# Attention heads one by one, or in pairs with wider operations

## The reference, cut to what matters

```
s = jnp.einsum('bqkgd,bskd->bkgqs', qi, ki).astype(F32) * scale
s = jnp.where(mi[None, None, None], s, -jnp.inf)
sink_col = jnp.broadcast_to(sink[None, :, :, None, None], s.shape[:-1] + (1,))
p = jax.nn.softmax(jnp.concatenate([s, sink_col], axis=-1), axis=-1)[..., :-1]
return jnp.einsum('bkgqs,bskd->bqkgd', p.astype(vi.dtype), vi)
```

## Time and profile before

| | |
|---|---|
| median of 3 runs | 1547.64 us |
| profiled execution, time | 1549.7 us |
| its span, first to last instruction | 1547.9 us |
| mean granted clock of TensorE | 0.962 |
| busy share of the span | PE 96%, PEld 81%, DVE 83%, ACT 64%, POOL 4% |
| attention, first score matmul to first matmul of the output projection | 458.81 to 510.34 us |

### The profile page before, as it was taken

How to read it: one execution, slowest core, us unless ns; L and a number is a source line. 1 busy time by engine, 2 the same in 40 slices (tenths; PEclk the granted TensorE clock), 3 DMA queues, 4 the chain that set the end, 5 groups by cost and what they waited for, 6 DMA issues and landing times.

```text
span 1547.9 us, 19150 instructions
## 1 busy us (share of the span) xinstructions
PE 1489.5 (96%) x7536; PEld 1247.8 (81%) x7537; DVE 1290.3 (83%) x1542; ACT 991.1 (64%) x1191; POOL 62.8 (4%) x57
## 2 busy tenths in 40 slices
PE   7998899999889979999999999999999999999996
PEld 5887799999545868888888888888888888888885
DVE  5488798988558448799999999999999999999995
ACT  2152344344327248788888888888888888888884
POOL 0000000000000030001001001001001000000001
PEclk7799999999988969999999999999999999999998
DMA  9875969989640529999999999999999999999980
GB/s 341 300 253 198 327 228 313 326 312 329 217 179 1 181 78 350 373 330 361 393 383 364 395 384 354 397 386 369 391 386 366 385 392 361 384 395 375 375 300 16
DMA packets 222159, 485.46 MB, mean 314 GB/s; under 512 B 6160, under 2 KB 33008, under 8 KB 222064
## 3 DMA queue, kind: packets, MB, share of 16 engines
q1 hardware_dynamic: 217296, 474.04, 83.5%
q0 software_dynamic: 2160, 7.87, 2.0%
q10 hardware_dynamic: 2608, 2.27, 0.4%
HBM read 477.86 MB, written 6.29 MB: 313 GB/s over the span
## 4 chain that ended last, share of the span: by engine, by line
issue 51%; PE 38%; DVE 6%; POOL 3%; ACT 1%; DMA 0%; ACTq 0%; DVEq 0%; POOLq 0%
PE bank L1534 5%; PE bank L1535 4%; PE bank L1536 4%; PE bank L1728 3%; PE bank L1729 3%; PE bank L1730 3%; PE bank L1459 2%; PE bank L1442 2%; PE bank L1594 2%; PE bank L1426 1%; POOL y L598 1%; PE bank L1411 1%; PE bank L1357 1%; PE bank L1401 1%; POOL out L602 1%
## 5 line engine op out<-in xcount | busy, mean ns | idle before, releaser
L1298 DVE TENSOR_TENSOR wlo<-ring,whi 128x1024 fp32r<-128x1024 f32 x672 | 815.1, 1236 | 77.8 <-ACT whi L858 55.9
L858 ACT ACTIVATE whi<-ring 128x1024 fp32r<-128x1024 f32 x672 | 711.7, 1062 | 178.5 <-PE bank L1730 178.3
L1728 PE MATMUL bank<-whi,xh 128*128 128x512 f32 x904 | 360.3, 399 | 4.2 <-DVE wlo L1298 3.9
L1730 PE MATMUL bank<-wlo,xh 128*128 128x512 f32 x904 | 354.3, 392 | 0.0
L1729 PE MATMUL bank<-whi,xl 128*128 128x512 f32 x904 | 353.8, 391 | 0.0
L1728 PEld LDWEIGHTS bank<-whi,xh 128*128 128x128 f32 x904 | 170.7, 189 | 41.3 <-issue 7.8
L1730 PEld LDWEIGHTS bank<-wlo,xh 128*128 128x128 f32 x904 | 170.7, 189 | 36.7
L1729 PEld LDWEIGHTS bank<-whi,xl 128*128 128x128 f32 x904 | 171.1, 189 | 33.9
L1728 PE MATMUL bank<-whi,hh 128*128 128x512 f32 x440 | 172.0, 391 | 0.0
L1730 PE MATMUL bank<-wlo,hh 128*128 128x512 f32 x440 | 171.3, 389 | 0.0
L1729 PE MATMUL bank<-whi,hl 128*128 128x512 f32 x440 | 171.2, 389 | 0.0
(11 more groups left out here) (254 smaller groups left out, 1671.1 us busy)
## 6 DMA issues: line engine op xcount, KB each, us to landing
ring<-in_m_w_gu SPq DMA_DIRECT2D x112, 2048.0 KB, 10.9
ring<-in_m_w_down SPq DMA_DIRECT2D x56, 2048.0 KB, 10.5
ring<-in_ada_w SPq DMA_DIRECT2D x24, 2048.0 KB, 12.8
ring<-in_f_w_gu SPq DMA_DIRECT2D x24, 1024.0 KB, 14.1
ring<-in_f_w_down SPq DMA_DIRECT2D x6, 2048.0 KB, 14.4
ring<-in_a_w_in SPq DMA_DIRECT2D x4, 2048.0 KB, 17.2
ring<-in_kv_ada_w SPq DMA_DIRECT2D x4, 2048.0 KB, 13.1
ring<-in_a_w_out SPq DMA_DIRECT2D x2, 2048.0 KB, 10.3
```

The source lines that it names most:

```text
L858: nc.scalar.activation(whi[:, n % WB, :], moe_raw(n), ACT.Copy).then_inc(hi_ready, 1)
L1298: v_.tensor_tensor(wlo[:, n % WB, :], moe_raw(n), whi[:, n % WB, :].bitcast(F32), ALU.subtract).then_inc(lo_ready, 1)
L1728: mm(o, hi, whi[:, b, c0:c0 + 512], start=start, stop=False)
L1730: return mm(o, hi, wlo[:, b, c0:c0 + 512], start=False, stop=stop)
```

## The change

Heads are handled in pairs, p = 0 to 7. Each DVE `scores` of a pair is four `tensor_tensor_reduce` (scale, mask and running maximum with the sink as the start value, straight from PSUM), one negation and one addition of the sinks for both heads; `probs` is four instructions for both heads, the multiplications as `tensor_tensor` with the reciprocal broadcast. DVE's order is `probs(p)`, `scores(p+2)`, then the copy of `values(p-1)`, which moves from ACT to DVE. ACT does the four exponentials of a pair without waits between them, one sink exponential and one copy of 768 columns from two banks. PE issues four `keep_clock` ahead of the scores of each pair, also ahead of the first, then the four score matmuls with the two heads (two halves of the partitions, two banks) taking turns; the `keep_clock` between scores and transposes are gone. `Pb` becomes three buffers of a pair, `PT` moves into `G`, and the transposes have one pair of banks (4, 5), so `probs_T(p)` waits for `copy_p(p-1)`. Scores use banks 0 to 3, values banks 6 and 7.

The diff, with its added lines; what they replace are the functions printed above:

```diff
@@ -128,7 +128,8 @@
...
+        psum = ctx.enter_context(nc.psum_tensor("psum", [P, 8, 512], F32))
+        bank = [psum[:, i, :] for i in range(8)]
...
@@ -168,7 +169,10 @@
...
+        flat = lambda t: t[:, :, :].rearrange("p k n -> p (k n)")
+        Pb = [part.rearrange("p (b n) -> p b n", b=2) for part in (
+            flat(Dd)[:, 0:6 * P], flat(Dd)[:, 6 * P:12 * P], flat(C)[:, 0:6 * P])]
+        PT = flat(G)[:, 0:12 * P].rearrange("p (b n) -> p b n", b=4)
...
@@ -500,6 +505,8 @@
...
+        score_bank = lambda p, j: bank[2 * (p % 2) + j]
...
@@ -761,35 +768,30 @@
...
+            ex, pt = Signal(exp_done), Signal(pT_evac)
+            def exps(p):
+                act.wait_ge(nm_done, p + 1)
+                for j in range(2):
+                    h = 2 * p + j
+                    nc.scalar.activation(Pb[p % 3][:, j, 0:P], Pb[p % 3][:, j, 0:P], ACT.Exp, bias=nm[:, h, 0:1],
+                                         accum_out=sm[:, h, 0:1])
+                    nc.scalar.activation(Pb[p % 3][:, j, P:3 * P], Pb[p % 3][:, j, P:3 * P], ACT.Exp,
+                                         bias=nm[:, h, 1:2], accum_out=sm[:, h, 1:2])
+                act.wait_ge(es_set, p + 1)
+                then(nc.scalar.activation(es[:, 2 * p:2 * p + 2, :], es[:, 2 * p:2 * p + 2, :], ACT.Exp), ex)
+            def copy_p(p):
+                act.wait_ge(pT_mm, p + 1)
+                if p >= 2:
+                    act.wait_ge(pv_mm, p - 1)
+                then(nc.scalar.activation(PT[:, 2 * (p % 2):2 * (p % 2) + 2, :], psum[:, 4:6, 0:3 * P], ACT.Copy), pt)
...
+            for p in range(NH // 2):
+                if p + 1 < NH // 2:
+                    exps(p + 1)
+                copy_p(p)
...
@@ -1179,32 +1181,48 @@
...
+            sce, nms, ess, pns, oe = (Signal(sc_evac), Signal(nm_done), Signal(es_set), Signal(pn_done),
+                                      Signal(o_evac))
+            def scores(p):
+                dve.wait_ge(sc_mm, p + 1)
+                if p >= 3:
+                    dve.wait_ge(pT_mm, p - 2)
+                pair = slice(2 * p, 2 * p + 2)
+                for j in range(2):
+                    h = 2 * p + j
+                    for c0, c1, i in ((0, P, 0), (P, 3 * P, 1)):
+                        ins = v_.tensor_tensor_reduce(out=Pb[p % 3][:, j, c0:c1], in0=score_bank(p, j)[:, c0:c1],
+                                                      in1=mask[:, c0:c1], scale=HD ** -0.5, scalar=sinks[:, h:h + 1],
+                                                      op0=ALU.add, op1=ALU.max, accum_out=mx[:, h, i:i + 1])
+                then(ins, sce)
+                then(v_.tensor_scalar(nm[:, pair, :], mx[:, pair, :], -1.0, None, ALU.mult), nms)
+                then(v_.tensor_tensor(es[:, pair, :], nm[:, pair, :], sinks[:, pair][:, :, None].to_broadcast([P, 2, 2]),
+                                      ALU.add), ess)
+            def probs(p):
+                pair = slice(2 * p, 2 * p + 2)
+                dve.wait_ge(exp_done, p + 1)
+                then(v_.tensor_tensor(sm[:, pair, :], sm[:, pair, :], es[:, pair, :], ALU.add))
+                then(v_.reciprocal(sm[:, pair, :], sm[:, pair, :]))
+                for c0, c1, i in ((0, P, 0), (P, 3 * P, 1)):
+                    ins = v_.tensor_tensor(Pb[p % 3][:, :, c0:c1], Pb[p % 3][:, :, c0:c1],
+                                           sm[:, pair, i:i + 1].to_broadcast([P, 2, c1 - c0]), ALU.mult)
+                then(ins, pns)
+            def copy_o(p):
+                dve.wait_ge(pv_mm, p + 1)
+                then(v_.tensor_copy(A[:, p, :], bank[6 + p % 2][:, 0:SEQ]), oe)
+            for p in range(2):
+                scores(p)
+            for p in range(NH // 2):
+                probs(p)
+                if p + 2 < NH // 2:
+                    scores(p + 2)
+                if p:
+                    copy_o(p - 1)
+            copy_o(NH // 2 - 1)
...
@@ -1597,49 +1615,55 @@
...
+            def scores(p):
+                if p >= 2:
+                    pe.wait_ge(sc_evac, p - 1)
...
+                g = 2 * p // (NH // NKV)
+                keep_clock(score_bank(p, 0)[:, :], 4)
+                for j in range(2):
+                    lo = HD * j
+                    mm(score_bank(p, j)[:, 0:P], B[lo:lo + HD, p, 0:P], kT[lo:lo + HD, g, 0:P], start=True, stop=True)
+                for j in range(2):
+                    lo = HD * j
+                    last = mm(score_bank(p, j)[:, P:3 * P], B[lo:lo + HD, p, P:2 * P], kT[lo:lo + HD, g, :], start=True,
+                              stop=True)
+                last.then_inc(sc_mm, 1)
+            def probs_T(p):
+                pe.wait_ge(pn_done, p + 1)
+                if p:
+                    pe.wait_ge(pT_evac, p)
+                for j in range(2):
+                    for i in range(3):
+                        last = transposed(bank[4 + j][:, i * P:(i + 1) * P], Pb[p % 3][:, j, i * P:(i + 1) * P],
+                                          ident[:, :])
...
+            def values(p):
+                pe.wait_ge(pT_evac, p + 1)
+                if p >= 2:
+                    pe.wait_ge(o_evac, p - 1)
+                g = 2 * p // (NH // NKV)
...
+                for j in range(2):
+                    o = bank[6 + p % 2][HD * j:HD * j + HD, :]
+                    p_ = PT[:, 2 * (p % 2) + j, :]
+                    mm(o[:, 0:P], v0, p_[:, 0:P], start=True, stop=True)
+                    mm(o[:, P:2 * P], v0, p_[:, P:2 * P], start=True, stop=False)
+                    last = mm(o[:, P:2 * P], v1, p_[:, 2 * P:3 * P], start=False, stop=True)
+                last.then_inc(pv_mm, 1)
+            for p in range(2):
+                scores(p)
+            for p in range(NH // 2):
+                if p + 2 < NH // 2:
+                    scores(p + 2)
+                probs_T(p)
+                if p:
+                    values(p - 1)
+            values(NH // 2 - 1)
...
```

More of the change, by code:

```diff
@@ L130, in build @@
         tok_i = sb("tok_i", [P, NB, E], I32)
-        bank = [ctx.enter_context(nc.psum_tensor(f"bank{i}", [P, 512], F32)) for i in range(8)]
+        psum = ctx.enter_context(nc.psum_tensor("psum", [P, 8, 512], F32))
+        bank = [psum[:, i, :] for i in range(8)]
         with ExitStack() as region:
@@ L762, in _ @@
             copy_T(5)
-            ex, pt, oe = Signal(exp_done), Signal(pT_evac), Signal(o_evac)
-            def exps(h):
-                act.wait_ge(nm_done, h + 1)
-                then(nc.scalar.activation(Pb[:, h % 4, 0:P], Pb[:, h % 4, 0:P], ACT.Exp, bias=nm[:, h, 0:1],
-                                          accum_out=sm[:, h, 0:1]))
-                then(nc.scalar.activation(Pb[:, h % 4, P:3 * P], Pb[:, h % 4, P:3 * P], ACT.Exp, bias=nm[:, h, 1:2],
-                                          accum_out=sm[:, h, 1:2]))
-                then(nc.scalar.activation(es[:, h, :], nm[:, h, :], ACT.Exp, bias=sinks[:, h:h + 1]), ex)
@@ L774, in copy_p @@
-            def copy_p(h):
-                act.wait_ge(pT_mm, h + 1)
-                if h >= 2:
-                    act.wait_ge(pv_mm, h - 1)
-                then(nc.scalar.activation(PT[:, h % 2, 0:3 * P], bank[7 if h % 2 else 4][:, 0:3 * P], ACT.Copy), pt)
-            def copy_o(k):
-                act.wait_ge(pv_mm, 2 * k + 2)
-                then(nc.scalar.activation(A[:, k, :], bank[k % 2][:, 0:SEQ], ACT.Copy), oe)
-            exps(0)
-            exps(1)
-            for h in range(NH):
-                if h + 2 < NH:
-                    exps(h + 2)
-                copy_p(h)
-                if h >= 2 and h % 2 == 0:
-                    copy_o(h // 2 - 1)
@@ L1180, in _ @@
                     ada(25)
-            sce, nms, pns = Signal(sc_evac), Signal(nm_done), Signal(pn_done)
-            def scores(h):
-                dve.wait_ge(sc_mm, h + 1)
-                if h >= 4:
-                    dve.wait_ge(pT_mm, h - 3)
-                p_ = Pb[:, h % 4, :]
-                then(v_.scalar_tensor_tensor(out=p_, in0=bank[5 + h % 2][:, 0:3 * P], scalar=HD ** -0.5,
-                                             in1=mask[:, :], op0=ALU.mult, op1=ALU.add), sce)
-                then(v_.tensor_reduce(mx[:, h, 0:1], p_[:, 0:P], AX.X, ALU.max))
-                then(v_.tensor_reduce(mx[:, h, 1:2], p_[:, P:3 * P], AX.X, ALU.max))
-                then(v_.tensor_scalar(nm[:, h, :], mx[:, h, :], sinks[:, h:h + 1], -1.0, ALU.max, ALU.mult), nms)
@@ L1204, in _ @@
-            for h in range(NH):
-                if h + 2 < NH:
-                    scores(h + 2)
-                probs(h)
+            sce, nms, ess, pns, oe = (Signal(sc_evac), Signal(nm_done), Signal(es_set), Signal(pn_done),
[15 more added lines that the diff above has]
+                                      ALU.add), ess)
@@ L1611, in probs_T @@
-            def probs_T(h):
-                pe.wait_ge(pn_done, h + 1)
-                if h >= 2:
-                    pe.wait_ge(pT_evac, h - 1)
-                b = bank[7 if h % 2 else 4]
```

(27 more changed lines are left out.)

21 lines of the change are left out of this document (2 added, 19 removed).

## The result

The changed kernel takes 1538.85 us, median of 4 runs (1537.40 to 1540.58), and the kernel before, with one more run beside it, 1547.91 us (median of 4, 1545.77 to 1550.51). The ratio is 0.9941, 95% interval 0.9922 to 0.9961: faster by 9.1 us, where 2.3 was forecast. The profiled execution took 1537.86 us (span 1536.1, mean granted clock 0.967).

What follows compares the result with a forecast made beforehand. DVE was taken to set attention's pace, PE close behind. Five middle pairs gain 0.9 us each (5.5 to 4.6), the start gives part back: 1547.64 - 2.3 = 1545.3 us, range 1542 to 1550.5.

Steps and rivals of the forecast that it cites:

- the exchange rate: Attention against the whole kernel: a shorter attention makes the kernel shorter one for one, and a longer one longer.
- The prediction's own sign of being wrong: Wrong if the pair period is not 4.4 to 4.9 us, the clock rises after 475, or the experts begin unexpectedly late.
- both engines want 4.6 us: Steady attention: DVE needs 4.57 us and PE 4.58 us a pair, where the pair took 5.5.
- PE's sum: PE per pair at 2.4 GHz: dummies 0.88, scores 1.5, transposes 0.76, values 1.44, sum 4.58 us against 5.0 before.
- The overlap rival: Score matmuls of two heads overlap, hiding 0.43 us a pair: gain 3.7 us, 4.9 with cheap or no read; chance 0.28.
- DVE's sum: DVE per pair: scores 2.55, `probs` 1.56, copy 0.46, sum 4.57 us; 4.17 with no accumulator read, 4.92 with the dear one.
- the rival with the dear accumulator read: DVE's 32 reductions: each 0.1 us of read beyond 0.10 costs up to 3.2 us; chance 0.17.
- 4.17: DVE's sum in us a pair if the reductions' maximum costs no accumulator read.
- The clock: PE's granted clock at attention's start: rise taken at 466.7 us; at 463.3 gains 0.3 more, at 473.5 costs 1.4.
- Clock stays low: Rival in the first pairs: a late rise makes it slower, by 1.5 us at 480.3 and 4.9 at 487; chance 0.17.
- Behind attention: After attention nothing changes; DVE's 4.4 us chunk stays covered by the projection; without that cover it costs up to 4.4.
- The ring of waits: Through PE and DVE: values, copy 0.46, `probs` 1.56, transposes 0.76, values 1.44, handover 0.2: 4.42 us, just below both engines.

Runs made afterwards that it cites:

- values in turns: Changed kernel with a pair's six value matmuls alternating between the two heads instead of three and three: 1536.05 us, ratio to before 0.9930.
- the copy later: Changed kernel with DVE's order probabilities of p, copy of the values of p-2, scores of p+2: 1534.65 us, ratio to before 0.9921.
- the extra dummies: Changed kernel plus six more dummy matmuls ahead of the transposes of pair 0 and of the last two pairs: 1537.61 us, ratio to before 0.9933.

## Why the prediction was wrong

The stage and the direction were right, and so was the exchange rate: over the 16 profiles attention runs from 38.3 to 55.3 us, and the span without it stays at 1489.7 to 1496.4 and does not follow it. The prediction's own sign of being wrong, a period outside 4.4 to 4.9 us, came true. Time from PE's first instruction in attention, by its stations:

| | predicted | measured | gained |
|---|---|---|---|
| first reduction | 4.9 | 3.64 | 1.3 |
| `probs(0)` | 11.4 | 8.72 | 2.7 |
| `probs(1)` | 15.5 | 12.07 | 3.4 |
| `probs(6)` | 38.7 | 32.86 | 5.8 |
| `probs(7)` | 43.2 | 37.52 | 5.7 |
| end of the last copy | 49.1 | 43.66 | 5.5 |

**The step that failed is "both engines want 4.6 us"**: both sums were 0.8 us too high, each for its own reason, and the period is 4.01 us instead of 4.62. Neither sum alone would have moved it. With the scores apart and DVE as changed it is 4.66 to 4.68, with the scores overlapped and DVE at 5.4 it is 5.39, and by the forecast's own rule an overlap with DVE at 4.57 would have left 4.6.

**PE's sum**, "scores twice 0.85 less one change 0.1 to 0.2, so 1.5" and "values 0.70 + 0.74 = 1.44 ... Sum 4.58", counts the passes of two heads one after the other. As changed, PE needs 0.97 + 0.9 + 0.81 + 1.08 = 3.8 us. This sum alone gives the 1.3 us at the first reduction.

**The overlap rival** had the right mechanism and the wrong size. It hid one pass at each change of head, 0.43 us a pair and 0.9 at the start, and only in the scores. Measured are 0.6 us in the scores (a whole head hides), 0.36 in the values, and 1.3 at the start. The rule cited for it, from the Trainium skill ("TensorEngine Tiling (Array Packing)", "Key Properties"), the trace bears out, for tiles that split the rows and for tiles that split the columns.

**DVE's sum** was 0.8 us too high (3.77 instead of 4.57), and the rival with the dear accumulator read fell. Of that 0.6 are the four reductions. The durations 0.35, 0.48, 0.42, 0.16 were right. Taken wrongly was that durations add up: back to back an instruction costs 0.07 to 0.08 us less than it lasts, and the read, put at 0.10, is part of that. By the Trainium skill's rule ("VectorE: DVE Perf Modes", "Two Vector instructions with no wait between them") I called 4.17 out of reach. The trace does show two instructions (0.083 us for the read), but together they advance the queue by less than the first one's duration. This term gives 0.7 us before `probs(0)` and 0.75 before `probs(1)`. In the steady part it alone would have given nothing, as said above.

**ACT**: exponentials without waits come 0.40 and 0.49 us apart, 1.77 for four instead of 2.2, and the sinks 0.19 instead of 0.33: 0.6 us, on the path only at the start. The last 0.1 before `probs(0)` is that the forecast let it wait for `scores(1)`.

**The clock** rose 4.7 us after the first dummy, not 7.9, and it goes with the overlap of the scores: in the ten kernels that have it, the rise comes 4.2 to 4.8 us after PE's first instruction of attention, in the other six 14.6 to 25.1. It dropped again at 468.6 and at the end, which the prediction did not have. `probs(7)` to the last copy took 6.14 us instead of 5.95. "Clock stays low" was not this kernel's fate, but a real one: with the heads' scores apart it happened, and with dummies between them the time was the one of before.

**Behind attention**, "nothing changes" held, and the lost cover of DVE's chunk cost nothing: DVE then still waits 1.30 us for PE before the first residual. The ring of waits was forecast "just below" both engines, at 4.42. With both engines at 3.8 it is the bound, at 0.42 + 0.04 + 1.44 + 0.05 + 0.81 + 1.08 + 0.17 = 4.0.

## What to carry to other kernels

When a change puts small matmuls of different rows or columns of the array next to each other, price them once as a sum and once as the longer of the two, and ask what the rest would then be bound by. Count an instruction in a row without waits by the distance between starts, not by its duration. When two engines both get cheaper, look at the ring of waits between them, and at what the same order costs where the work runs out: here one line moved in DVE's order took 5.2 us off attention, 1.3 by the ring and the rest at the end, a third of the whole change again in the ratios (0.9921 against 0.9941).

## What the hardware showed that was not expected

- Half-height matmuls of two heads run fully at once: 1.58 us for two heads at 1.2 GHz where one takes 1.57. It holds as well when one head's are issued as a block ahead of the other's (0.9 us for a pair at 2.4 GHz both ways). A wait between them takes it away (1.83 us). The half-width ones take 1.73 us one by one, 1.08 in two blocks of three and 0.80 in turns.
- The granted clock followed the overlap. With two heads' scores at once it rose 4.7 us after PE's first instruction (4.2 to 4.8 in ten kernels). With one at a time, and PE busy 9.88 of 10 us, it rose 17.9 us after it (14.6 to 25.1 in six). What in the activity decides, these runs do not show.
- Whether the clock drops at the end of attention differs between kernels that are nearly alike there: in the changed kernel it did (0.66 in 490 to 500 us), with waits after the reductions, values in turns or the copy later it did not. With the extra dummies it stayed up as well. Why the others differ stays open.
